# Layer 1's modulation is computed between the expert slots of two sample blocks, and not beside the last block

## The reference, cut to what matters

```python
def trunk_layer(x, cond, lp, rope, ctx):
    m = jnp.einsum('bsd,df->bsf', jax.nn.silu(cond), lp['w_ada']) + lp['b_ada']   # 1024 -> 6*1024
    sh1, sc1, g1, sh2, sc2, g2 = jnp.split(m, 6, axis=-1)
    mix, ctx_out = mixer(rmsnorm(x, lp['norm1_g']) * (1 + sc1) + sh1, lp, rope, ctx)
    x = x + g1 * mix
    hff = rmsnorm(x, lp['norm2_g']) * (1 + sc2) + sh2
    return x + g2 * peer_ffn(hff, ...), ctx_out

def one(hb):                       # peer_ffn, for each block of 128 tokens
    ...                            # each token chooses 8 heads x 16 of 16384 experts
    act = jax.nn.gelu(jnp.einsum('thkd,td->thk', u_tab[idx], hb), approximate=False)
    return jnp.einsum('thk,thkd->td', gate * act, v_tab[idx])
```

## Time and profile before

| | us |
|---|---|
| median of 3 runs | 5076.69 (5076.66 to 5082.86) |
| the profiled execution, its own time | 5067.13 |
| its span in the trace | 5065.3 |
| PE / DVE / ACT / POOL busy | 3905.9 / 3247.4 / 743.5 / 1442.1 |
| mean granted clock of PE | 0.918 |

### The profile page before, as it was taken

The page is one execution under the profiler, slowest core; times in us unless marked ns, Lnnn a source line. Parts: engine busy times, 40 slices in busy tenths (PEclk is TensorE's granted clock), DMA queues, the critical chain, the costliest instruction groups (busy, mean ns, idle before and its releaser), DMA issues. The chain is left out here.

```text
span 5065.3 us, 36421 instructions
## 1 busy us (share of the span) xinstructions
PE 3905.9 (77%) x11046; PEld 1925.4 (38%) x11046; DVE 3247.4 (64%) x8263; ACT 743.5 (15%) x2205; POOL 1442.1 (28%) x1284
## 2 busy tenths in 40 slices
PE   7479577889777777778868776789987777777776
PEld 6365233554223222235535632346432322222222
DVE  1534866644887867854474648664468787687666
ACT  0121124311101001010022111341111100100101
POOL 0001122211444444432222011222134444344432
PEclk9689688999998999999989887899999999999999
DMA  8244346763998998999959334567469999899998
GB/s 262 71 131 142 140 174 225 260 220 128 404 418 362 421 421 365 421 395 390 371 205 355 135 125 159 205 237 259 156 252 421 388 401 421 366 421 421 415 421 343
DMA packets 342149, 1497.72 MB, mean 296 GB/s; under 512 B 31424, under 2 KB 176448, under 8 KB 178112
## 3 DMA queue, kind: packets, MB, share of 16 engines
q0 software_dynamic: 184320, 1342.26, 66.2%
q1 hardware_dynamic: 157632, 153.13, 9.4%
HBM read 1491.97 MB, written 3.31 MB: 295 GB/s over the span
## 5 line engine op out<-in xcount | busy, mean ns | idle before, releaser
L650 PE MATMUL expert_acc<-uv_ring,diag 128*128 128x512 f32 x3744 | 1895.4, 640 | 430.1 <-DVE diag L1207 420.7
L604 POOL DMA_INDIRECT uv_ring<-uv,expert_index x936 | 1051.9, 1124 | 2816.8 <-PE expert_acc L650 2249.1
L650 PEld LDWEIGHTS expert_acc<-uv_ring,diag 128*128 128x128 f32 x3744 | 702.1, 201 | 1515.1 <-DVE diag L1207 898.2
L1198 DVE CUSTOM_DVE_ANT_0 uv_ring<-uv_ring,arena 128x1024 f32<-128x1024 f32 x680 | 832.0, 1224 | 236.9 <-DMA uv_ring<-uv,expert_index 234.1
L650 PE MATMUL expert_acc<-arena,diag 128*128 128x512 f32 x1376 | 692.4, 636 | 258.1 <-DVE diag L1207 189.8
L1207 DVE TENSOR_SCALAR diag<-const_mats,expert_gate,gelu 128x128 f32<-128x128 f32 x1280 | 465.4, 364 | 372.9 <-ACT gelu L929 276.4
L929 ACT ACTIVATE gelu<-u_dot 128x1 f32<-128x1 f32 x1280 | 256.3, 203 | 2995.9 <-DVE u_dot L1198 2991.9
L604 POOL DMA_INDIRECT arena<-uv,expert_index x344 | 390.0, 1134 | 763.6 <-PE expert_acc L650 465.2
L1198 DVE CUSTOM_DVE_ANT_0 arena<-arena 128x1024 f32<-128x1024 f32 x344 | 420.9, 1224 | 174.1 <-DMA arena<-uv,expert_index 172.4
L650 PEld LDWEIGHTS expert_acc<-arena,diag 128*128 128x128 f32 x1376 | 248.6, 197 | 692.9 <-DVE diag L1207 403.4
L1198 DVE CUSTOM_DVE_ANT_0 uv_ring<-uv_ring,prompt_rows 128x1024 f32<-128x1024 f32 x256 | 312.2, 1220 | 86.8 <-DMA uv_ring<-uv,expert_index 86.1
(11 more groups left out here) (201 smaller groups left out, 2788.3 us busy)
## 6 DMA issues: line engine op xcount, KB each, us to landing
w_ring<-w_ada SPq DMA_DIRECT2D x66, 512.0 KB
w_ring<-w_in SPq DMA_DIRECT2D x64, 512.0 KB
w_ring<-w_pq SPq DMA_DIRECT2D x64, 512.0 KB
w_ring<-w_out SPq DMA_DIRECT2D x32, 512.0 KB
uv_ring<-w_ada SPq DMA_DIRECT2D x30, 512.0 KB, 6.0
uv_ring<-uv,expert_index POOLq DMA_INDIRECT x936
arena<-b_ada SPq DMA_DIRECT2D x48, 128.0 KB
arena<-uv,expert_index POOLq DMA_INDIRECT x344
```

The source lines that it names most:

```text
L604: pool.indirect_dma_start(out=UV[j], out_offset=None, in_=uv, in_offset=bass.IndirectOffsetOnAxis(ap=idxs[:, n % 2, k:k + 1], axis=0)).the ...
L650: ins = pe.matmul(acc[:, half, :], diag[:, m % DIAGS, :], UV[SLOT_AT[m]][:, D + 512 * half:D + 512 * half + 512], start=(k == 0), stop=(k ...
L1198: V_.tensor_tensor_reduce(UV[j][:, 0:D], UV[j][:, 0:D], rows_of(n), 1.0, 0.0, ALU.mult, ALU.add, dots[:, m % DOTS:m % DOTS + 1]).then_inc( ...
```

## The change

Layer 1's modulation moves to an earlier place: the 24 units stand between the slots of sample blocks 2 and 3 of layer 0, twelve in each, after slots 5, 15, ... 115. `mod_unit_at` says where. Four things go with it.

- The bias is a ninth product on PE: the 24 bias rows lie in a tile `bada` of 24 partitions, loaded once per layer with 24 KB, and a column of the identity matrix picks the row. The loads of the spread rows are gone, in both layers.
- ACT drains the modulation (`modulate` on ACT), in both layers, where DVE did.
- In layer 1 SP issues the modulation's weights right behind the last loads of layer 0's sample mixer. Each waits for its buffer.
- `BESIDE_PROMPT` has no entries for the modulation. Its 128 slots stand beside the prompt mixer alone, more at each point up to pq.

`add_peer`, which adds the expert sum to `x`, now writes its product back to PSUM and no longer to `psum_out`; that frees room in the arena for `mrow`, the row tiles. A few one-element copies and the table of small integers for `choose` move to other tiles.

The diff, cut to its core; behind the tables stand SP's part, PE's and ACT's, in this order.

```diff
+MOD_GROUPS = [[x for x in mod_steps() if x[0] == "mod" and x[1] == u or x[0] == "modT" and x[2] + 1 == u] for u in range(ADA_UNITS)]
+MOD_GROUPS[-1] += [x for x in mod_steps() if x[0] == "modT" and x[2] + 1 == ADA_UNITS]
+
+def mod_unit_at(l, b, k):
+    return (b - 1) * ADA_UNITS // 2 + k // 10 if l + 1 < L and b in (1, 2) and k % 10 == 5 and k < 5 * ADA_UNITS else None
...
-BESIDE_PROMPT = points(("mod", range(24), 2), ("n1", [1], 3), ("pa", range(2), 2), ("pz", range(2), 2), ("px", range(6), 1),
-                       ("pg", range(4), 1), ("conv", [5], 2), ("taps", range(4, 30, 5), 1), ("cT", [0], 2), ("st", range(2), 3),
-                       ("yT", [0], 2), ("v", [0], 2), ("head", range(6), 2), ("wo", range(4), 2), ("n2", [1], 3),
-                       ("pq", range(16), 1))
+BESIDE_PROMPT = points(("n1", [1], 8), ("pa", range(2), 5), ("pz", range(2), 3), ("px", range(6), 3), ("pg", range(4), 3),
+                       ("conv", [5], 4), ("taps", range(4, 30, 5), 3), ("cT", [0], 4), ("st", range(2), 5), ("yT", [0], 4),
+                       ("v", [0], 4), ("head", range(6), 2), ("wo", range(4), 2), ("n2", [1], 4), ("pq", range(16), 1))
...
                 if l:
+                    sp.wait_ge(*full["mod"].at(l - 1, 0, ADA_UNITS - 1))
+                sp.dma_start(bada[0:ADA_UNITS, :], b_ada[l].rearrange("(u n) -> u n", n=WU)).then_inc(s_brow.sem, 16)
+                for u in range(ADA_UNITS):
+                    load_w(w_unit(l, 0, "ada", u), w_ada[l, :, u * WU:(u + 1) * WU])
...
+            def modulate(l, unit):
+                if unit == 0:
+                    pe.wait_ge(*s_cond.at(l))
+                    pe.wait_ge(*s_brow.at(l))
+                for s, i, u in MOD_GROUPS[unit]:
+                    t = fill(s, l, 0, i)
                     if s == "mod":
                         w = weights(l, 0, "ada", u)
                         for c in range(DC):
+                            pe.matmul(t[:, 0:WU], hT[:, c, 0:P], w[:, c, :], start=(c == 0), stop=False)
+                        ins = pe.matmul(t[:, 0:WU], C[0:ADA_UNITS, C_ID, u:u + 1].broadcast_to([ADA_UNITS, P]), bada[0:ADA_UNITS, :],
+                                        start=False, stop=True)
...
                         for k in range(SLOTS):
                             add_v(n, k)
+                            unit = mod_unit_at(l, b, k)
+                            if unit is not None:
+                                modulate(l + 1, unit)
...
+                    elif u // 4 in (2, 5):
+                        col = (u % 4) * WU
+                        for k in range(2):
+                            for q in range(2):
+                                ins = nc.scalar.activation(G[64 * q:64 * q + 64, gate_tile(l, u // 12, k), col:col + WU],
+                                                           t[64 * k:64 * k + 64, 0:WU], ACT.Copy)
+                    else:
+                        turned = sum(1 for x in mod_steps() if x[0] == "modT" and x[2] < u)
+                        if turned >= 2:
+                            act.wait_ge(*full["modT"].at(l, 0, turned - 2))
+                        ins = nc.scalar.activation(mrow[turned % 2], t[:, 0:WU], ACT.Copy)
...
                         for k in range(SLOTS):
                             gelu(n, k)
+                            unit = mod_unit_at(l, b, k)
+                            if unit is not None:
+                                modulate(l + 1, unit)
```

More of the change, by code:

```diff
@@ L209, in psum_order @@
     for l in range(L):
-        out += [(s, l, 0, i) for s, i, _ in mod_steps()]
+        if l == 0:
+            out += [(s, 0, 0, i) for s, i, _ in itertools.chain(*MOD_GROUPS)]
         for g in range(2):
@@ L239, in psum_order @@
             out += [("pq", l, g, i) for i in range(8, 16)] + [("ps", l, g, 2), ("ps", l, g, 3)]
-            for b in range(1, nb):
-                out += [("ht", l, g, 2 * b), ("ht", l, g, 2 * b + 1)]
-                out += [("ps", l, g, 4 * b + i) for i in range(4)]
+            for b in range(nb):
+                if b + 1 < nb:
+                    out += [("ht", l, g, 2 * b + 2), ("ht", l, g, 2 * b + 3)]
+                    out += [("ps", l, g, 4 * b + 4 + i) for i in range(4)]
+                if g:
+                    units = [mod_unit_at(l, b, k) for k in range(SLOTS)]
+                    out += [(s, l + 1, 0, i) for u in units if u is not None for s, i, _ in MOD_GROUPS[u]]
     return out
@@ L317, in build @@
         xn = [at(k * D, D) for k in range(2)]
-        mrow = [at(2048 + k * WU, WU) for k in range(2)]
-        brow = [at(2560 + k * WU, WU) for k in range(2)]
+        mrow = [at(15812 + k * WU, WU) for k in range(2)]
         def mixer_tiles(g):
@@ L405, in build @@
         s_lw = Stage("layer_weights_loaded", (1, 0), 16 * 3)
-        s_brow = [Stage(f"b_ada_row_loaded{k}", (ADA_UNITS // 2, 0), 16) for k in range(2)]
+        s_brow = Stage("b_ada_rows_loaded", (1, 0), 16)
         s_condt = Stage("cond_tanh", (1, 0))
@@ L933, in gelu_beside, with cond, modulate @@
                     gelu(n, m)
+            def cond(l):
+                nc.scalar.activation(sc_c[:, 1], sc_c[:, 0], ACT.Tanh, scale=0.5).then_inc(s_condt.sem, 1)
+                chain(nc.scalar.activation(aneg[:], pr[:, l, slice(*PAR["alog"])], ACT.Exp))
+            def modulate(l, unit):
+                for s, i, u in MOD_GROUPS[unit]:
+                    t = tile_of(s, l, 0, i)
+                    if s == "modT":
+                        k = 2 * (u % 4)
+                        which = {0: 0, 1: 1, 3: 2, 4: 3}[u // 4]
+                        ins = nc.scalar.activation(modc[:, which, k:k + 2, :],
+                                                   t[:, 0:2 * P].rearrange("p (k m) -> p k m", k=2)[:, :, 0:P:64], ACT.Copy)
+                    elif u // 4 in (2, 5):
[9 more added lines that the diff above has]
+                        ins = nc.scalar.activation(mrow[turned % 2], t[:, 0:WU], ACT.Copy)
+                    ins.then_inc(free[s].sem, 1)
             beside = Beside(gelu_beside)
-            act.wait_ge(s_const.sem, 16 * 7)
+            act.wait_ge(s_const.sem, 16 * 8)
             act.wait_ge(s_x.sem, 16)
             for l in range(L):
-                nc.scalar.activation(sc_c[:, 1], sc_c[:, 0], ACT.Tanh, scale=0.5).then_inc(s_condt.sem, 1)
-                chain(nc.scalar.activation(aneg[:], pr[:, l, slice(*PAR["alog"])], ACT.Exp))
-                for u in range(ADA_UNITS):
-                    beside.point("mod", u)
+                if l == 0:
+                    cond(0)
+                    for u in range(ADA_UNITS):
+                        modulate(0, u)
                 for g in range(2):
@@ L1221, in add_peer, with cond @@
                 ins.then_inc(s_pup.sem, 1)
+            def cond(l):
+                if l:
+                    dve.wait_ge(*full["ht"].at(l - 1, 1, 1))
+                dve.wait_ge(*s_condt.at(l))
+                chain(V_.scalar_tensor_tensor(sc_c[:, 1], sc_c[:, 1], 1.0, sc_c[:, 0], ALU.add, ALU.mult))
+                chain(V_.tensor_scalar(sc_c[:, 1], sc_c[:, 1], 0.5, None, ALU.mult))
+                for k in range(2):
+                    ins = V_.tensor_copy(hT[:, :, 64 * k:64 * k + 64], sc_c[:, 1, :, k:k + 1].broadcast_to([P, DC, 64]))
+                ins.then_inc(s_cond.sem, 1)
             def dot_beside(n, m):
```

103 lines of the change are left out of this document (32 added, 71 removed).

## The result

The changed kernel takes 5095.3 us in the median of 8 runs (5084.6 to 5100.6), the kernel before 5078.8 us of 8 (5069.0 to 5086.1) on the same chip. The ratio is 1.0031, 95% interval 1.002 to 1.0042: **slower by 0.31%**, some 16 us, where 5057 was forecast in a range of 5025 to 5090. The profiled executions have spans of 5093.3 and 5065.3 us. They are 28 us apart, more than the medians, since the profiled execution of before, at 5067.1 us, is a fast one of its kind.

The account below looks back on a forecast made before the run. DMA was taken as the main bound, with pauses in layer 1's prompt mixer. Terms -201 + 84 + 105 - 8 = -20 us took the median of 5076.7 to 5057, range 5025 to 5090.

Parts of the forecast that it names:

- The prompt mixer has 48 slots more: Layer 1's prompt mixer: 48 added slots, priced by what binds in each window, cost +105 us, 349 then 454.
- st, yT and v: Windows of layer 1's prompt mixer, a chain of short steps: 8 added slots at 2.0 us, +16 us.
- Full DMA: Windows pz, px and pg of layer 1's prompt mixer: DMA binds, 22 added slots at 2.49 us, +53 us.
- three signs of being wrong: A block over 375 us, DMA share in pz, px and pg under 0.95, or the prompt mixer under 435 us.
- The blocks, +84: Sample blocks 2 and 3 of layer 0: twelve units each, +78 us of DMA and +6 for hand-overs.
- The price of a unit, 3.25 us: Sample blocks 2 and 3: DMA time of one unit's weights, 1.05 MB; ten slots and a unit take 28.15 us.
- The detour of 7.4 us: Sample blocks 2 and 3: serial path over PE and ACT between diagonals at a unit; fits with 0.6 us to spare.
- second rival: Sample blocks 2 and 3: the detour over ACT binds; at 10.4 us the kernel is slower, 5089 us; chance 0.21.
- Layer 0, -8: Layer 0's modulation: early ACT drains and no spread bias loads save 8 us, between -2 and -12.
- The removed stage, -201: Layer 1's modulation stage vanishes from its old place: -201 us, including 9.8 us of bias rows.
- The mixer at 1.78 us a slot: Rival: layer 1's prompt mixer hides slots as well as before, 48 slots cost +85, 5037 us; chance 0.20.
- That nothing comes of it: Rival: DMA binds throughout, mixer idle time stays 63 us, work only moves, 5070 us; chance 0.17.

Follow-up runs that it names:

- front48: The changed kernel with 48 slots of layer 0's sample block 4 done alone ahead of layer 1's prompt mixer, then the old table: 5083.1 us, 1.002 of the kernel before.
- ring4: The changed kernel with four instead of five gather buffers for layer 0's sample block 4: 5165.1 us, 1.0191 of the kernel before.
- ring6: The changed kernel with six instead of five gather buffers for layer 0's sample block 4, same table: 5040.0 us, 0.9931 of the kernel before.

## Why the prediction was wrong

- **The failing step is "The prompt mixer has 48 slots more", +105.** It was 153. The prices in it (2.49 us where DMA binds, 1.7 in the taps, 2.0 in st, yT and v) assume that a slot's rows are there when its point comes. I had looked at the buffers for the blocks (eight or nine) and not for block 4 (five, two of them held at every point). What the runs showed in its place: with five buffers a slot of block 4 costs 3.0 us even alone (front48), and 70 us of mixer more or 52 less come with one buffer fewer or more (ring4, ring6). With a sixth buffer the same table costs +101. That this meets the +105 is in part luck: up to the first product of the attention's heads (2658.1 us before, 2654.1 in ring6) it is +128 where +117 were forecast, behind it -27 where -12 were. Measured against forecast: first window +28 (+21), pz, px, pg +69 (+53), conv, taps, cT +36 (+27), st, yT, v +40 (+16), n2 +2 (+2), pq -18 or, to the same event, -24 (-14). The worst is st, yT and v, where helpings of 4 and 5 follow long stops.
- **"Full DMA" read off a share.** My test for pz, px and pg was a share of at least 0.95. It was 0.98, and it passed; the price was off all the same, 370 GB/s for 406 with one buffer more. None of the three signs of being wrong came (the blocks took 361 and 357 us, the mixer 507): for the mixer I had named only a time that is too short.
- **The blocks, +84, measured +70.** The price of a unit, 3.25 us, held: 28.0 us for ten slots where 28.15 were forecast. Three of the 24 units had been loaded long before block 2, at 1207 us, which makes 21 x 3.25 = 68. The detour of 7.4 us was well counted too: from one diagonal's end to the next it measures 7.2 to 7.4 us at most units of the first 80 slots, 8.4 at the gate units. The first unit of a block cost more, 11 us with 8.4 of waiting. TensorE had just idled 17 us, its granted clock was 0.50 (1.2 GHz) from 1590 to 1601 us, and its first slot took 3.78 us for 1.98. The slot, and the window:

```profile
1597.94 3.78 PE L659 MATMUL expert_acc<-arena,diag 128*128 128x512 f32 x4 [16.68 <-DVE x L1268]
```

```profile
1590.00:1601.00 11.00, 3.06 (x4) 1.51 (x5) 8.64 (x19) 0.79 (x4) 1.59 (x2) 0.50 1.01 422
```

That the detour would bind only beyond 0.6 us of margin, the second rival's condition, came true beside choosing, but it was worth nothing by itself, as the bytes stood right behind it. This rival did not decide the outcome. Its 5089 is the number nearest to the 5095 measured, and that is luck: it wanted a detour of 10.4 us and +116 in the blocks.
- **Layer 0, -8, measured +0.5.** The ninth product was priced at an eighth of eight, 0.45; with the two changes of height it takes 0.78 (4.45 less the 3.67 from one unit to the next without it before, 49.17 to 52.84). ScalarE's early drains did remove the waits for the bias (TensorE is busy 39.0 of the 39 us from 21 to 60, 26.9 before) and the product ate the gain: 24 x 0.33 = 8.
- **The removed stage, -201, was right** (-204).
- **The rivals.** The mixer at 1.78 us a slot (5037) was the wrong way; with six buffers it is 101 / 48 = 2.1, so even then the added slots are dearer than the first ones. That nothing comes of it (5070) has the right direction, for a reason other than it gave: the idle time did not stay at 63 us but grew to 91.

## What to carry to other kernels

When work is spread between the steps of a chain, the size of a helping has to be compared with the number of buffers that are free at that moment: count those still held by the lag of a later engine, and price what exceeds it by the wait until a freed buffer is filled again (3.65 and 2.39 us in the timeline above), not by the transfers' bandwidth. A DMA share near 1 in a stretch does not say that the stretch is at its bandwidth: look at the GB/s against the best stretch of the same transfers. When two limits lie within a few per cent of each other, taking one away shows little of its price (3 and 18 us here); take both (51).

## What was not expected of the hardware

- A product over 24 rows between products over 128 stops the overlap of TensorE's weight loads on both sides, 0.33 us each, and is slower than one over 128 rows with 104 rows of zero weights (4.45 and 4.11 us a unit). The Trainium skill, TensorE: Matmul & The Clock Gate, Part 3, The mechanism, lists that a weight load overlaps running products only where the row group differs, and says above this that one into the background weight buffer is pulled ahead too; in this trace all 128-row loads overlap and those at the change of height don't.
- Gathers of 8 KB rows ran at 421 GB/s with eight or nine buffers and at 345 alone with five, without any other work beside them (front48).
- The share of busy DMA time stayed at 0.97 to 1.01 in 1590 to 1830 whether ten slots took 28 us with a unit's weights (407 GB/s) or with a quarter of them (384 GB/s).
